# Down products of two SwiGLU blocks by Strassen's seven block products, with block sums on GpSimd, in a one-core decoder layer

## The chip, the cores and the metric

One NeuronCore of one Trainium2 chip. The metric is device microseconds (us) of one execution, input load and output store included. TensorE is called PE, VectorE DVE, ScalarE ACT, GpSimd POOL; SP issues the weight DMAs.

## What is computed

One layer on 256 tokens, width 1024, all float32: `x += 0.5*SwiGLU(RMSNorm(x))`, then a mixer (one input projection, 8 attention heads, 16 state-space heads, an output projection), then again `x += 0.5*SwiGLU(RMSNorm(x))` and a final RMSNorm. The part that changes is

```python
def swiglu(h, w1, w3, w2):
    return (jax.nn.silu(h @ w1) * (h @ w3)) @ w2
```

with h 256x1024, w1 and w3 1024x2816, w2 2816x1024, which runs twice (FFN n = 0 and 1, called FFN 1 and 2 in the text).

## The kernel before

**Products in three parts.** Every large product keeps float32 accuracy by splitting both operands in a high part (type fp32r) and the rest: `three` (L1112) issues hi*hi, hi*lo and lo*hi into one PSUM bank. So a weight that was loaded goes through two engines: ACT writes `w_hi` as a copy with the rounding type (`split_hi`, L453), DVE writes `w_lo` as raw minus high part (`split_lo`, L769), and `half_ready` counts the finished halves (128x1024 each), which PE waits for.

**Tiles and loops.** The 2816 hidden columns are 22 f-tiles of 128, taken in 11 pairs i = 0 to 10, odd = 0 or 1 within a pair. Three loads of 1 MB belong to a pair: w1 (kind 0), w3 (kind 1), w2 (kind 2), each into its own one of three raw slots (`ffn_load`, L268), issued on SP's queue in the order kind 0, 1, 2 and each once the second half that last lay in that slot is split. For f-tile (i, odd) PE computes gate and up, transposed, as 8 contraction tiles x 3 matmuls of 256 columns each (`gate_or_up`, L1149), into two banks: gate in bank 4, up in bank 5. ACT takes the silu of gate (`gate`, L500), DVE multiplies by up (`up`, L826), ACT and DVE split the product into `gu_hi` and `gu_lo`. PE then adds the f-tile's down product (`down`, L1133): two token tiles t x two column halves c, 3 matmuls of 512 columns each, accumulated in banks 0 to 3 over all 22 f-tiles. Pair 0 is different: both its f-tiles are computed with tokens on partitions (`pair_product`), multiplied, and transposed by PE (`pair_transposes`).

**Order of the work.** It is written out by hand on each engine; between engines there are only semaphores. PE does gate, up of one f-tile, then the down product of the f-tile before it (L1211 to L1217 is the loop over i). ACT and DVE run one `ffn_step` (L510, L837) for each f-tile: the splits of the next f-tile's w1 and w3, then silu and multiply, then the split of w2's half. A gate product waits only for its weights and for the silu before to have left bank 4.

On ACT:

```python
def ffn_step(n, i, odd):
    i2, odd2 = (i, 1) if not odd else (i + 1, 0)
    ffn_hi(n, i2, odd2, 0)
    ffn_hi(n, i2, odd2, 1)
    gate(n, i, odd)
    act.wait_ge(down_done, (FT - 1) * n + 2 * i + odd)
    ffn_hi(n, i2, odd2, 2)
```

At the end of an FFN `update_x` (L783, DVE) adds half of each finished bank to x. POOL does only small work: the norms' `rsqrt` (L363), nine parameter loads (L408 to L416) after the sixth down product, softplus, rotary products, and a 128x512 product in the mixer (L431).

## Time and profile before

| | |
|---|---|
| runs before | 572.85, 573.39, 572.8 us, median 572.85 |
| the profiled execution | 573.44 us, its span 571.7 us |
| PE busy | 553.1 us, 97% of the span |
| DVE, ACT, POOL busy | 324.1, 288.8, 49.3 us |
| DMA | 98.14 MB, mean 172 GB/s |

The profile is of one execution. The span runs from its first to its last instruction; 1.7 us of the execution's time lie outside. A row of a timeline gives start, duration, engine, line of the kernel, operation, output and inputs, and in brackets how long the engine sat idle before and who released it. PE's matmuls overlap, so the distance of starts, not the duration, is a matmul's price.

### The profile page before, as it was taken

To read this page: it belongs to the slowest core of one execution; us is meant where nothing else is said; L and a number is where in the kernel's file an instruction comes from. 1 tells how busy PE (TensorE), PEld (TensorE's weight loads), DVE (VectorE), ACT (ScalarE), POOL (GpSimd) and SP (SyncE) were. 2 spreads that over 40 slices of the span, in tenths; PEclk is the share of its full clock that TensorE was granted. 3 is DMA by queue.
4 is the path that set the end of the run, shared out by engine and by line. 5 is a ranking of instruction groups with operands and counts; after the bars stand their busy time and mean duration, and the time that the engine had idled before them with its cause. 6 is when DMAs were issued, how large, how long until landed. Compare 5 with 4: busy or idle time off the path is not lost.

```text
span 571.7 us, 9567 instructions
## 1 busy us (share of the span) xinstructions
PE 553.1 (97%) x3736; PEld 508.1 (89%) x3736; DVE 324.1 (57%) x450; ACT 288.8 (51%) x463; POOL 49.3 (9%) x86
## 2 busy tenths in 40 slices
PE   5999999999999999999999999999999999999994
PEld 4999999999999979998889688789999999999993
DVE  3655554554554684877766666575554544554544
ACT  4544453444443464866675874364453444443433
POOL 1000040000000020412431102010000000000001
PEclk9999999999999999999999999999999999999998
DMA  8935497655457637565323235253466655456601
GB/s 246 330 109 197 154 288 277 205 163 173 151 189 221 218 123 214 159 209 163 134 77 145 73 111 175 84 169 125 162 209 220 204 163 174 150 189 220 220 1 74
DMA packets 69448, 98.14 MB, mean 172 GB/s; under 512 B 1828, under 2 KB 55264, under 8 KB 69424
## 3 DMA queue, kind: packets, MB, share of 16 engines
q1 hardware_dynamic: 68576, 95.34, 51.7%
q0 software_dynamic: 848, 2.47, 1.5%
q8 instruction: 16, 0.26, 0.2%
q14 instruction: 8, 0.07, 0.0%
HBM read 96.75 MB, written 1.05 MB: 171 GB/s over the span
## 4 chain that ended last, share of the span: by engine, by line
PE 89%; DVE 4%; ACT 3%; DMA 1%; issue 1%; POOL 1%; SPq 0%; POOLq 0%; DVEq 0%; ACTq 0%
PE bank L1114 28%; PE bank L1115 27%; PE bank L1116 27%; DMA raw<-in_ffn_w 1%; PE bank L1239 1%; ACT decay L649 1%; DVE w_lo L775 1%; ACT z_silu L481 1%; ACT w_hi L457 1%; POOL mean_sq L368 1%; DVE x L787 1%; PE bank L1388 1%; PE bank L1387 1%; PE bank L1374 1%; DVE normed L992 0%
## 5 line engine op out<-in xcount | busy, mean ns | idle before, releaser
L775 DVE TENSOR_TENSOR w_lo<-raw,w_hi 128x1024 fp32r<-128x1024 f32 x176 | 211.1, 1228 | 146.0 <-ACT w_hi L457 145.5
L457 ACT ACTIVATE w_hi<-raw 128x1024 fp32r<-128x1024 f32 x176 | 179.6, 1054 | 114.6 <-PE bank L1116 73.2
L1114 PE MATMUL bank<-hT_hi,w_hi 128*128 128x256 f32 x736 | 208.5, 283 | 0.0
L1116 PE MATMUL bank<-hT_hi,w_lo 128*128 128x256 f32 x736 | 208.3, 283 | 0.0
L1115 PE MATMUL bank<-hT_lo,w_hi 128*128 128x256 f32 x736 | 208.2, 283 | 0.0
L1114 PEld LDWEIGHTS bank<-hT_hi,w_hi 128*128 128x128 f32 x736 | 141.1, 192 | 1.5
L1115 PEld LDWEIGHTS bank<-hT_lo,w_hi 128*128 128x128 f32 x736 | 141.1, 192 | 1.5
L1116 PEld LDWEIGHTS bank<-hT_hi,w_lo 128*128 128x128 f32 x736 | 141.1, 192 | 0.0
L1114 PE MATMUL bank<-w_hi,hT_hi 128*128 128x512 f32 (+1 forms) x192 | 70.1, 365 | 0.8 <-DVE w_lo L775 0.5
L1114 PE MATMUL bank<-w_hi,gu_hi 128*128 128x512 f32 x176 | 69.2, 393 | 0.3
L1115 PE MATMUL bank<-w_lo,gu_hi 128*128 128x512 f32 x176 | 69.0, 392 | 0.0
L1116 PE MATMUL bank<-w_hi,gu_lo 128*128 128x512 f32 x176 | 68.5, 389 | 0.0
L1116 PE MATMUL bank<-w_hi,hT_lo 128*128 128x512 f32 (+1 forms) x192 | 68.3, 356 | 0.0
L1115 PE MATMUL bank<-w_lo,hT_hi 128*128 128x512 f32 (+1 forms) x192 | 68.1, 354 | 0.0
L508 ACT ACTIVATE gu_hi<-gu 128x256 fp32r<-128x256 f32 x40 | 16.7, 418 | 89.1 <-DVE gu L832 83.4
L1114 PEld LDWEIGHTS bank<-w_hi,hT_hi 128*128 128x128 f32 x192 | 36.3, 189 | 7.7 <-issue 2.0
L1116 PEld LDWEIGHTS bank<-w_hi,hT_lo 128*128 128x128 f32 x192 | 36.3, 189 | 5.4
L1115 PEld LDWEIGHTS bank<-w_lo,hT_hi 128*128 128x128 f32 x192 | 36.3, 189 | 4.3
L1116 PEld LDWEIGHTS bank<-w_hi,gu_lo 128*128 128x128 f32 x176 | 33.1, 188 | 7.2
L1114 PEld LDWEIGHTS bank<-w_hi,gu_hi 128*128 128x128 f32 x176 | 33.2, 189 | 6.8 <-issue 1.1
L1115 PEld LDWEIGHTS bank<-w_lo,gu_hi 128*128 128x128 f32 x176 | 33.2, 189 | 5.3
L368 POOL TENSOR_SCALAR mean_sq<-sumsq 128x1 f32<-128x1 f32 x8 | 4.8, 596 | 346.6 <-ACT z_silu L481 346.6
(164 smaller groups left out, 413.6 us busy)
## 6 DMA issues: line engine op xcount, KB each, us to landing
raw<-in_ffn_w SPq DMA_DIRECT2D x63, 1024.0 KB, 5.5
raw<-in_w_in SPq DMA_DIRECT2D x16, 1024.0 KB, 5.6
raw<-in_w_out SPq DMA_DIRECT2D x6, 1024.0 KB, 4.9
raw<-in_ffn_w SPq DMA_DIRECT2D x6, 512.0 KB, 7.4
x<-in_x SPq DMA_DIRECT2D x4, 256.0 KB, 4.0
out_x<-normed SPq DMA_DIRECT2D x4, 256.0 KB, 2.0
norm_w<-in_ffn_norm SPq DMA_DIRECT2D x1, 512.0 KB, 6.3
norm_w<-in_mix_norm POOLq DMA_DIRECT2D x1, 512.0 KB, 6.4
```

Of the source, the lines that this page charges most:

```text
L368: step(pool.tensor_scalar(m, sumsq[:, 0, col:col + 1], sumsq[:, 1, col:col + 1], EPS, ALU.add, ALU.add))
L457: act.activation(by_tile(dst) if columns else dst, src, ACT.Copy).then_inc(hi_ready, 1)
L481: act.activation(z_silu[:, t, cols], x[:, t, cols], ACT.Square, scale=D ** -0.5, accum_out=sumsq[:, c, r:r + 1]).then_inc(sq_ready, 1)
L508: act.activation(gu_hi[:, odd, :], gu[:, :], ACT.Copy).then_inc(gu_hi_ready, 1)
L649: act.activation(probs[:, h % 2, a:b], probs[:, h % 2, a:b], ACT.Exp, bias=row_bias[:, h, t:t + 1], scale=HD ** -0.5, accum_out=row_sum[:, ...
L775: dve.tensor_tensor(lo, src, hi, ALU.subtract).then_inc(half_ready, 1)
L787: dve.scalar_tensor_tensor(xs, bank[:, 2 * t + c, :], 1.0 if n == 2 else 0.5, xs, ALU.mult, ALU.add).then_inc(x_ready, 1)
L1114: pe.matmul(dst, lhs[0], rhs[0], start=start, stop=False, skip_group_check=True)
L1115: pe.matmul(dst, lhs[0], rhs[1], start=False, stop=False, skip_group_check=True)
L1116: return pe.matmul(dst, lhs[1], rhs[0], start=False, stop=stop, skip_group_check=True)
L1239: last = pe.transpose(bank[:, bank_n, k * P:(k + 1) * P], normed[:, t, col + k * P:col + (k + 1) * P], ident)
L1374: pe.matmul(b[:, 0:384], select_r[:, h:h + 1].to_broadcast([P, P]), csT[:, :], start=True, stop=False, skip_group_check=True)
```

## The change

For the first ten pairs of an FFN, the pair's down product is seen as a 2x2 block product: A11, A12, A21, A22 (token tile t x f-tile, 128x128 each, out of `gu`) times B11, B12, B21, B22 (f-tile x 512 columns, out of w2). Strassen's scheme in Winograd's form needs seven block products instead of eight, with four sums of A blocks (S1 to S4) and four of B blocks (T1 to T4). The eleventh pair keeps eight products.

- POOL computes T1 to T4 out of the raw w2 tile once it is loaded (`pair_sums`, 128x512 each, T2 after T1, T4 after T2) and S1 to S4 out of `gu` (`operand_sums`, 128x128 each).
- ACT and DVE split what enters the products: B11 with B21 (`left`), T4 (`sum4`), T1 to T3 (`sums`), B22 (`corner`), S1 to S4 (`asum`). w1 and w3 are split as before; w2's halves only for the last pair.
- PE adds the seven products of all ten pairs into banks 4, 0, 1, 2, 5, 6, 7. Gate and up now share bank 3: a gate product waits until DVE has multiplied the f-tile before it (`gu_ready`), and the silu waits for up. Down products run in two parts (`down_first`: 3 products, `down_second`: 4), a pair late.
- The w2 load of a pair waits for `corner_ready` of the pair before; SP's loop issues the two loads of pair i+1, then w2 of pair i.
- At the end the seven sums are folded: a copy of one bank on ACT, four half-bank steps on DVE, and four additions to x on POOL (`fold`), while PE does the last pair. `update_x` waits for `folded` as well.
- POOL's nine parameter loads stand behind the sums of the second pair. `xbc`, `qT`, `kT` share memory with the new tiles; `gu`, `w2_sum` and `asum` lie in tiles of the mixer.

```diff
-PAIR_ORDER = ((0, 0), (0, 1), (1, 0), (1, 1), (0, 2), (1, 2))
+PAIR_ORDER = ((0, 0), (0, 1), (1, 0), (1, 1))
+PAIRS = FI - 1
+P_BANK = {1: 4, 2: 0, 3: 1, 4: 2, 5: 5, 6: 6, 7: 7}
+GU_BANK = 3
...
+            def w2_load(n, i):
+                sp.wait_ge(corner_ready, i + PAIRS * n)
+                ffn_load(sp, n, i, 2)
...
+                gate_up_loads(n, 1)
+                with sp.Fori(1, FI - 1) as i:
+                    gate_up_loads(n, i + 1)
+                    w2_load(n, i)
...
+            def pair_sums(n, i):
+                p, w = PAIRS * n + i, w2_blocks(n)
+                pool.wait_ge(raw_loaded[(FFN_UNIT0[n] + 2) % RAW_SLOTS], w2_count(n, i))
+                if not (isinstance(p, int) and p == 0):
+                    pool.wait_ge(sums_ready, p)
+                    pool.wait_ge(sum4_ready, p)
+                pool.tensor_tensor(w2_sum[:, T1, :], w[:, 1, :], w[:, 0, :], ALU.subtract).then_inc(sum_done, 1)
+                pool.wait_ge(sum_done, p * 4 + 1)
+                pool.tensor_tensor(w2_sum[:, T2, :], w[:, 3, :], w2_sum[:, T1, :], ALU.subtract).then_inc(sum_done, 1)
+                pool.wait_ge(sum_done, p * 4 + 2)
+                pool.tensor_tensor(w2_sum[:, T4, :], w[:, 2, :], w2_sum[:, T2, :], ALU.subtract).then_inc(sum_done, 1)
+                pool.tensor_tensor(w2_sum[:, T3, :], w[:, 3, :], w[:, 1, :], ALU.subtract).then_inc(sum_done, 1)
...
+            def silu(n, i, odd):
+                f = looped(n, i, odd)
+                act.wait_ge(up_done, f + 1)
+                act.activation(silu_g, bank[:, GU_BANK, 0:SEQ], ACT.Silu).then_inc(silu_ready, 1)
...
+            def ffn_step(n, i):
+                second_hi(n, i - 1)
+                act.wait_ge(gate_done, looped(n, i, 0) + 1)
+                ffn_hi(n, i + 1, 0, 0)
+                silu(n, i, 0)
+                ffn_hi(n, i + 1, 0, 1)
+                product_hi(n, i, 0)
+                left_hi(n, i)
+                sum4_hi(n, i)
+                act.wait_ge(gate_done, looped(n, i, 1) + 1)
+                ffn_hi(n, i + 1, 1, 0)
+                silu(n, i, 1)
+                ffn_hi(n, i + 1, 1, 1)
+                product_hi(n, i, 1)
...
                 ffn_hi(n, 1, 0, 1)
+                left_hi(n, 0)
                 act.wait_ge(pair_T, 2 * n + 2)
...
+                act.activation(gu_hi[:, :, :], both, ACT.Copy)
+                act.activation(gu, both, ACT.Copy).then_inc(pair_copied, 1)
+                sum4_hi(n, 0)
                 ffn_hi(n, 1, 1, 0)
                 ffn_hi(n, 1, 1, 1)
...
+            def ffn_step(n, i):
+                second_lo(n, i - 1)
+                ffn_lo(n, i + 1, 0, 0)
+                up_silu(n, i, 0)
+                ffn_lo(n, i + 1, 0, 1)
+                product_lo(n, i, 0)
+                left_lo(n, i)
+                sum4_lo(n, i)
+                ffn_lo(n, i + 1, 1, 0)
+                up_silu(n, i, 1)
+                ffn_lo(n, i + 1, 1, 1)
+                product_lo(n, i, 1)
...
             def gate_or_up(n, i, odd, kind):
...
+                if kind == 0 and not (isinstance(f, int) and f == 0):
+                    pe.wait_ge(gu_ready, f)
+                columns_product(slot, bank[:, GU_BANK, kind * SEQ:(kind + 1) * SEQ]).then_inc(up_done if kind else gate_done, 1)
+
+            def gate_up_down(n, i):
+                gate_or_up(n, i, 0, 0)
+                if isinstance(i, int) and i == 1:
+                    for t in range(TT):
+                        pair_transposes(n, t)
+                gate_or_up(n, i, 0, 1)
+                down_first(n, i - 1)
+                gate_or_up(n, i, 1, 0)
+                gate_or_up(n, i, 1, 1)
+                down_second(n, i - 1)
```

In the text, hi(i,odd,gate) and lo(i,odd,gate) are the splits of w1's half (i, odd) on ACT and DVE, gate(i,odd) is PE's product; a tile or function name with _hi or _lo is its split.

## Rows read from the trace of the kernel before

**Rows 1.** The page, busy time, share of the span and instructions of each engine.
```profile
PE 553.1 (97%) x3736; PEld 508.1 (89%) x3736; DVE 324.1 (57%) x450; ACT 288.8 (51%) x463; POOL 49.3 (9%) x86
```

**Rows 2.** The page, chain that ended last, share of the span by engine.
```profile
PE 89%; DVE 4%; ACT 3%; DMA 1%; issue 1%; POOL 1%; SPq 0%; POOLq 0%; DVEq 0%; ACTq 0%
```

**Rows 3.** Timeline of PE, second FFN, steady step: start us, us, instruction.
```profile
442.29 0.28 PE L1114 MATMUL bank<-hT_hi,w_hi 128*128 128x256 f32 x1
448.04 0.40 PE L1114 MATMUL bank<-w_hi,gu_hi 128*128 128x512 f32 x1
450.79 0.28 PE L1114 MATMUL bank<-hT_hi,w_hi 128*128 128x256 f32 x1
```

**Rows 4.** The page, costliest groups: line, engine, forms, count, busy us, mean ns, idle before.
```profile
L775 DVE TENSOR_TENSOR w_lo<-raw,w_hi 128x1024 fp32r<-128x1024 f32 x176 | 211.1, 1228 | 146.0 <-ACT w_hi L457 145.5
L457 ACT ACTIVATE w_hi<-raw 128x1024 fp32r<-128x1024 f32 x176 | 179.6, 1054 | 114.6 <-PE bank L1116 73.2
```

**Rows 5.** Instructions by line or tile: count, duration ns min/median/max, first and last start.
```profile
L832 DVE TENSOR_TENSOR gu<-bank,conv_acc x40: 417/425/425, 35.6 to 558.7; 128x256 f32<-128x256 f32 x40
L431 POOL TENSOR_TENSOR normed<-x_tok,small x4: 1042/1194/2022, 265.3 to 271.6; 128x512 f32<-128x512 f32 x4
L602 ACT ACTIVATE q_tok<-bank x2: 617/622/626, 273.6 to 274.1; 128x512 f32<-128x512 f32 x2
```

**Rows 6.** Timeline of SP's queue, second FFN: three weight loads issued.
```profile
446.20 0.37 SPq L280 DMA_DIRECT2D raw<-in_ffn_w  x1
447.18 0.37 SPq L280 DMA_DIRECT2D raw<-in_ffn_w  x1
453.55 0.37 SPq L280 DMA_DIRECT2D raw<-in_ffn_w  x1
```

**Rows 7.** DMA issues 446:447, 447:449, 449:454, in this order: KB, us to landing.
```profile
raw<-in_ffn_w SPq DMA_DIRECT2D x1, 1024.0 KB, 5.5
raw<-in_ffn_w SPq DMA_DIRECT2D x1, 1024.0 KB, 7.5
raw<-in_ffn_w SPq DMA_DIRECT2D x1, 1024.0 KB, 5.0
```

**Rows 8.** Timeline of DVE and POOL in the mixer.
```profile
294.60 1.34 DVE L775 TENSOR_TENSOR w_lo<-raw,w_hi 128x1024 fp32r<-128x1024 f32 x1
294.94 1.32 POOL L382 TENSOR_TENSOR k_tok<-k_tok,cst 128x128 f32<-128x128 f32 x1
299.21 0.53 POOL L382 TENSOR_TENSOR k_tok<-k_tok,cst 128x128 f32<-128x128 f32 x1
...
269.59 2.05 POOL L431 TENSOR_TENSOR normed<-x_tok,small 128x512 f32<-128x512 f32 x2 [2.93 <-ACT x_tok L622]
270.98 1.74 DVE L775 TENSOR_TENSOR w_lo<-raw,w_hi 128x1024 fp32r<-128x1024 f32 x1 [1.86 <-ACT w_hi L457]
```

**Rows 9.** Timeline of PE and ACT, first FFN: first pair, and its last matmul.
```profile
28.24 0.28 PE L1114 MATMUL bank<-hT_hi,w_hi 128*128 128x256 f32 x1
31.76 0.60 ACT L534 ACTIVATE gu_hi<-bank 128x512 fp32r<-128x512 f32 x1 [1.99 <-PE bank L1178]
34.43 0.40 PE L1114 MATMUL bank<-w_hi,gu_hi 128*128 128x512 f32 x1
...
204.30 0.39 PE L1116 MATMUL bank<-w_hi,gu_lo 128*128 128x512 f32 x1
```

**Rows 10.** The page, DMA queues: packets, MB, share of 16 engines.
```profile
q1 hardware_dynamic: 68576, 95.34, 51.7%
q0 software_dynamic: 848, 2.47, 1.5%
```

**Rows 11.** PE's last matmul, then two stretches (granted clock third from the end).
```profile
564.16 0.39 PE L1116 MATMUL bank<-w_hi,gu_lo 128*128 128x512 f32 x1
...
566.00:568.00 2.00, 0.00 (x0) 0.00 (x0) 1.16 (x3) 0.95 (x3) 1.39 (x2) 0.74 0.58 218
568.00:570.00 2.00, 0.00 (x0) 0.00 (x0) 0.20 (x1) 0.42 (x1) 0.00 (x0) 0.50 0.60 224
```

More of the change, by code:

```diff
@@ L418, in _ @@
+            fold(0)
             pool.wait_ge(scaled_right, 2)
@@ L519, in pair_silu, with last_step @@
+            def last_step(n):
+                i = FI - 1
+                second_hi(n, i - 1)
+                silu(n, i, 0)
+                product_hi(n, i, 0)
+                for j in range(2):
+                    last_hi(n, j)
+                fold_copy(n)
+                if n == 0:
+                    mix_hi(0)
+                silu(n, i, 1)
+                product_hi(n, i, 1)
             def pair_silu(n, t):
@@ L744, in _ @@
             norm_hi(2, 1)
-            for odd in range(2):
-                ffn_hi(1, 0, odd, 2)
             ffn_steps(1)
-            gate(1, FI - 1, 1)
             for c in range(2):
@@ L845, in pair_mul, with last_step @@
+            def last_step(n):
+                i = FI - 1
+                second_lo(n, i - 1)
+                up_silu(n, i, 0)
+                product_lo(n, i, 0)
+                for j in range(2):
+                    last_lo(n, j)
+                if n == 0:
+                    mix_lo(0)
+                up_silu(n, i, 1)
+                product_lo(n, i, 1)
+                fold_sums(n)
             def pair_mul(n, t):
@@ L1140, in down_both, with down_last @@
+            def down_last(n):
+                pe.wait_ge(last_ready, 2 * n + 2)
+                pe.wait_ge(gu_split, FT * (n + 1))
                 for t in range(TT):
                     for c in range(2):
-                        last = down(n, i, odd, t, c, start, False)
-                last.then_inc(down_done, 1)
-            def down_waits(n, i, odd):
-                pe.wait_ge(half_ready, ffn_half(n, i, odd, 2)[0] + 1)
-                pe.wait_ge(gu_split, FT * n + 2 * i + odd + 1)
+                        for j in range(2):
+                            slot = FFN_SLOT[n][j]
+                            last = three(bank[:, 2 * t + c, :], (gu_hi[:, j, tok(t)], gu_lo[:, j, tok(t)]),
+                                         tuple(w[:, slot, c * 512:(c + 1) * 512] for w in (w_hi, w_lo)),
+                                         t + c + 1 - j == 3, j == 1)
+                        last.then_inc(acc_ready, 1)
```

394 lines of the change are left out of this document (244 added, 150 removed).

## The prediction

> **What bounds the kernel now.** I read three views in this order. The page's busy shares put the matmul engine PE at 97% of the span, VectorE (DVE) at 57%, ScalarE (ACT) at 51%, GpSimd (POOL) at 9% [rows 1]; the chain of waits gives PE 89% of what ended last [rows 2]. So outside the norms the kernel is PE's own instruction stream. The PE timeline of one steady step gives its prices [rows 3]: from 442.29 to 448.04 two products (gate, up) of 24 matmuls of 256 columns run, so 2.875 us a product, 0.120 us a matmul; from 448.04 to 450.79 twelve matmuls of 512 columns, 0.229 us each. A pair of f-tiles is two such steps: 4 x 2.875 + 24 x 0.229 = 17.0 us. Everything else, 6 weight splits of 1.06 us on ACT and 1.23 us on DVE a pair [rows 4], hides under it.
>
> **What the change takes off PE.** Seven block products instead of eight, three matmuls each: 3 x 0.229 = 0.687 us less a pair, so 16.3 us. Ten pairs an FFN, two FFNs: -13.7 us. If nothing else moved, that were the result.
>
> **What it adds, and which ring it closes.** Per pair: on POOL four sums of 128x512 and four of 128x128; on ACT and DVE, for the two w2 halves split before, hi/lo splits of B11 with B21 (1024 columns), T4 (512), T1 to T3 (1536), B22 (512) and the operand sums (512). The nearest POOL row to a sum of 128x512 is a 128x512 product, 1.042 us at least and 1.19 in the median [rows 5]; I take 1.04, and keep 1.34 as the upper end for a sum with two full streams (below). Scaled by columns from 1.23, DVE gets 4 x 1.23 for gate and up, 4.9 for the new splits, 1.7 for two multiplies and two subtractions of 0.42 [rows 5]: 11.5 of 16.3 us. ACT fits as well. Busy time is thus no bound; order is.
>
> ACT's order in a step is: hi(i+1,0,gate), silu, hi(i+1,0,up), gu_hi, left_hi, sum4_hi, hi(i+1,1,gate), silu(i,1), and so on. sum4_hi waits for POOL's third sum T4, T4 for the w2 load of this pair, and everything behind it on ACT waits too, at last silu(i,1), whose multiply frees the one gate/up bank for gate(i+1,0). The loads are on one queue and every raw slot is single. The gate load i+2 is issued when lo(i+1,1,gate) is done, the up load a split later, the w2 load of i+1 when corner_lo of pair i is done, some 5 us on. In the trace the first two were issued at 446.20 and 447.18 [rows 6] and landed after 5.5 and 7.5 us [rows 7], at 451.7 and 454.7: they go one after the other, 3.0 us apart. A w2 load alone lands in 5.0 us [rows 7], so with the same start-up as the gate load (5.5 - 3.0 = 2.5) it moves for some 2.5 to 2.6 us; third in the stream, it lands 8.5 + 2.6 = 11.1 us after the gate load's issue. Then the ring, from the gate load's issue to the next one's: three loads 11.1; T1, T2, T4 in series with a semaphore between, 3 x 1.04 + 0.2 = 3.3; sum4_hi 0.6 [rows 5], less the overlap with its successor, 0.55; hi(.,1,gate) 1.06; lo 1.28 with its wait [rows 4]; issue 0.05. That is 17.3 us, and PE isn't in it. It is already longer than the 16.3 PE needs, and than the 17.0 of before, where the w2 split did not stand in front of a silu with POOL sums before it.
>
> **The port that POOL and DVE share.** left_lo, a DVE subtraction of two SBUF tiles, comes due just as T1 ends and T2 starts. The trace shows what two such instructions do side by side: a POOL 128x128 product took 1.32 us at 294.94, beside a DVE split that ran 294.60 to 295.94, and 0.53 us at 299.21; the other way round a DVE split took 1.74 us at 270.98 instead of 1.23, having waited for a POOL product that ended at 271.6 [rows 8]. One waits for the other to finish. So either T2 waits for left_lo or T4 does: 1.23 less some overlap, 1.0 us, and the ring is 18.3. The Trainium skill (SBUF — State Buffer, section on two separate sides) says that a DVE instruction with two SBUF inputs and a GpSimd instruction exclude each other for the whole instruction; by that rule the trace agrees, and the sum stays 18.3. The Trainium skill (GPSIMD Engine Reference, performance versus the Vector engine) gives 2.6 cycles an element at 1.2 GHz for two-input sums, an estimate of 1.11 us; with it the ring would be 0.2 us longer.
>
> Excess over PE's 16.3: 2.0 us in each of the 8 full rounds (from gate(2,0) to gate(10,0)): +16.0 an FFN.
>
> **The first step.** In FFN 1 gate(1,0) starts at 28.24 and the pair's transposed product is read by ACT at 31.76 [rows 9]. Behind it ACT now has a second copy, sum4_hi and hi(1,1,gate): 31.76 + 3 x 0.5 + 1.06, then lo 1.28: the next gate load is issued at 35.6, with the port 36.0, and lands at 41.5. hi(2,0,gate) stands on ACT ahead of silu(1,0), and lo ahead of the multiply on DVE: 41.5 + 1.06 + 1.28 + 0.4 + 0.15 = 44.4 before gate(1,1) may write the shared bank. PE, which reached its first down product at 34.43 [rows 9], is through nine matmuls at 36.5: 7.9 us idle, where before it had another bank. The third load of this stream lands at 47.1; 4.3 for three sums with the port, 0.55 + 1.06 + 1.28 + 0.57 put gate(2,0) at 54.9, 26.6 us after gate(1,0); PE's own work there (four products, 0.45 of transposes, 21 matmuls of 0.229) is 16.8. So +9.8.
> The last step costs +0.5 (all waits of the last down product now stand in front). The fold, four DVE steps of 0.7 and four POOL sums of 1.04, lies beside the last 5.5 us of down product and ends before the last block; cover gone, it would cost up to 2 us. It is taken at 0.
>
> Per FFN: -6.9 + 16.0 + 9.8 + 0.5 = +19.4; two, +38.8. An FFN lasts 176.3 us now (28.24 to 204.55 [rows 9]), so 195.7 after.
>
> **Smaller terms.** POOL's parameter loads move behind the second pair's sums into a stretch where weights stream: all of that queue's packets took 1.5% of 16 engines' span [rows 10], 8.6 us, about half of them these loads; +2, between 0 and 4.5. PE's clock: after the last matmuls at 564.2 the granted clock was 0.74 of 2.4 GHz in 566 to 568 and 0.50, so 1.2 GHz, after it [rows 11]. A gap of 7.9 us thus lowers it; one product at half rate (2.9 more) fits in the slack before silu(1,1) but for 0.3, two would cost 3.2. I take 0.5 each. The mixer is as before but for slots: 0.
>
> Sum against the profiled execution: 573.4 + 38.8 + 2 + 1 = 615.2; the median of the runs is 0.6 lower, so 614.6. I say **614**.
>
> **Rivals.** (A) The forecast, a ring of three loads, three sums and two splits with the port: 600 to 628, chance 0.57.
> (B) The port costs nothing on the ring, because the sums slip between splits or the sum stream holds it less: per FFN 8 x 1.0 + 0.8 less, so 614 - 17.6 = 596. Against it: both stretched rows. The range of this case is 586 to 600 (a load lands 0.4 us sooner: another -4 a FFN). The Trainium skill (Perfetto Trace Analysis, optimizing scalar/DVE operations) names only a 2-port DVE instruction as holder of the lock; a subtraction that were not one would give this 596, and [rows 8] speak against it. Chance 0.18.
> (C) Faster: the ring doesn't close, since loads and sums of a pair run ahead of PE; then PE's 16.3 stands and the time is 572.9 - 13.7 = 559. It decides at a ring of 16.3 (1.0 below my ring without the port) and a first gap under 6.9 us, which alone eats the saving; both have to give way. For it: the transfers are busy only half the time, 51.7% [rows 10]. Against: three single slots and the measured 5.5, 7.5 and 5.0 us. Chance 0.07 (with values between 559 and 571).
> (D) A sum with two full streams is dearer than the one of [rows 5]: 1.34 us instead of 1.04 adds 0.9 to each of nine rounds, +8 to 9 an FFN: 631. For it: the product's second input is one value repeated. Chance 0.16.
> (E) The saving and the waits cancel, or the change isn't what runs: 573, chance 0.02.
>
> **Numbers.** 614 is the likeliest case's. The range 591 to 631 holds most of A, B's centre and about half of D. A measurement of this kernel tells some 0.2% (1.1 us) from no change. Slower 0.92 (A, B, D and a bit), same 0.01, faster 0.07.
>
> **What the profile will show.** If right: PE idle in front of every gate(i,0), 1.5 us or more, released by DVE's multiply and behind it ACT's sum4_hi, POOL's T4 and a w2 load; rounds of 18.3 us; one gap near 8 us in each FFN's first step; w2 loads landing 6 us after issue; PE's share near 89%; POOL sums of 1.04 beside some of 2 us. Wrong if PE is still near 97%, if rounds are 16.3, if T1 starts well before ACT reaches left_hi, or if no POOL sum is stretched (then B).

## The result, and the profile after

The kernel with the block products takes 651.8 us (median of 4 runs, 648.72 to 654.32) where before takes 572.83 (572.77 to 573.39): a ratio of 1.137, 95% interval 1.132 to 1.142. The forecast was 614 with a range to 631: the direction is right, the size is not, and the measurement lies 21 us outside the range. The profiled execution took 652.08 us, with a span of 650.5.

The page of after; the first line answers to [rows 1], the shares of the chain to [rows 2], the last three lines are groups (count, busy us, mean ns, idle before):

```profile
PE 569.1 (87%) x3676; PEld 517.9 (80%) x3676; DVE 404.4 (62%) x518; ACT 334.1 (51%) x527; POOL 269.6 (41%) x254
PEclk9989899989989799999999999997988999889988
...
PE 28%; DVE 16%; issue 16%; POOL 16%; DMA 13%; ACT 9%; POOLq 0%; SPq 0%; ACTq 0%; DVEq 0%
...
L464 POOL TENSOR_TENSOR x_tok<-raw 128x512 f32<-128x512 f32 x20 | 25.9, 1294 | 138.2 <-DMA raw<-in_ffn_w 138.2
L628 ACT ACTIVATE w_hi<-x_tok 128x512 fp32r<-128x512 f32 x20 | 12.6, 632 | 71.6 <-POOL x_tok L468 71.6
L466 POOL TENSOR_TENSOR x_tok<-raw,x_tok 128x512 f32<-128x512 f32 x20 | 41.4, 2070 | 1.6
```

No engine is full, and the chain is spread over all of them: PE's part fell from 89% to 28%. That is the picture of a ring, a closed chain of waits in which the last link releases the first. x_tok holds the sums T1 to T4 here, v_tok holds gu. The waits of after (engine and line, what it waited for: us in total, times, longest us) name its links:

```profile
POOL x_tok L464 <- DMA raw<-in_ffn_w: 138.2, 19, 11.5
DVE w_lo L938 <- ACT w_hi L568: 73.1, 60, 3.2
ACT w_hi L628 <- POOL x_tok L468: 71.6, 18, 4.1
PE bank L1331 <- DVE v_tok L1039: 58.1, 20, 7.5
DVE w_lo L998 <- ACT w_hi L628: 57.8, 18, 3.2
```

T1 waits for the w2 load; sum4_hi (L628) waits for T4 (L468); and PE waits 20 times for DVE's multiply (L1039), once in front of every gate(i,0) from i = 2 on (0.8 to 4.0 us) and once in each first step (7.3 and 7.5 us).

One round of FFN 1, in order of time, from the timeline: ACT, DVE, POOL and the gate product's first matmul. The gate load was issued at 137.51, the up load at 138.82, the w2 load at 142.78; they landed after 5.6, 7.2 and 5.8 us, so the third at 148.58. The next gate load was issued at 156.66.

```profile
137.71 0.39 PE L1331 MATMUL bank<-hT_hi,w_hi 128*128 128x256 f32 x1 [4.01 <-DVE v_tok L1039]
139.67 2.07 DVE L1004 TENSOR_TENSOR sums_lo<-x_tok,sums_hi 128x1536 fp32r<-128x1536 f32 x1 [0.28 <-ACT sums_hi L636]
141.66 0.94 DVE L1007 TENSOR_TENSOR w_lo<-raw,w_hi 128x512 fp32r<-128x512 f32 x1
148.65 1.29 POOL L464 TENSOR_TENSOR x_tok<-raw 128x512 f32<-128x512 f32 x1 [6.58 <-DMA raw<-in_ffn_w]
149.69 1.33 DVE L993 TENSOR_TENSOR w_lo<-raw,w_hi 128x1024 fp32r<-128x1024 f32 x1 [0.96 <-ACT w_hi L621]
150.02 2.15 POOL L466 TENSOR_TENSOR x_tok<-raw,x_tok 128x512 f32<-128x512 f32 x1
152.25 1.29 POOL L468 TENSOR_TENSOR x_tok<-raw,x_tok 128x512 f32<-128x512 f32 x1
153.58 0.63 ACT L628 ACTIVATE w_hi<-x_tok 128x512 fp32r<-128x512 f32 x1 [3.91 <-POOL x_tok L468]
154.11 1.04 ACT L568 ACTIVATE w_hi<-raw 128x1024 fp32r<-128x1024 f32 x1
154.24 1.11 DVE L998 TENSOR_TENSOR w_lo<-x_tok,w_hi 128x512 fp32r<-128x512 f32 x1 [3.22 <-ACT w_hi L628]
155.28 1.21 DVE L938 TENSOR_TENSOR w_lo<-raw,w_hi 128x1024 fp32r<-128x1024 f32 x1
156.88 0.39 PE L1331 MATMUL bank<-hT_hi,w_hi 128*128 128x256 f32 x1 [1.10 <-DVE v_tok L1039]
```

This is the ring of the forecast, link by link: 11.07 us from the gate load's issue to the third landing, 4.96 to T4's end (153.54), then 3.12 for sum4_hi, sum4_lo, lo(.,1,gate) and the issue, together 19.15. This round is the shortest of FFN 1. Gate(2,0) to gate(10,0) is 56.43 to 217.88, 20.18 a round, and the three loads take 12.1 us in the mean of the eight (11.1 to 12.6). The rows on either side of T2 (L466) show the port: T2 took 2.15 where its neighbours took 1.29, beside left_lo (L993).

Two more places of after. The first step's gaps answer to [rows 9] (gate(1,1) and gate(2,0)), and the end of FFN 1 has the norm's transposes at 245.42, where before has them at 205.35:

```profile
44.66 0.55 PE L1331 MATMUL bank<-hT_hi,w_hi 128*128 128x256 f32 x1 [7.27 <-DVE v_tok L1039]
56.43 0.39 PE L1331 MATMUL bank<-hT_hi,w_hi 128*128 128x256 f32 x1 [0.96 <-DVE v_tok L1039]
...
217.88 0.55 PE L1331 MATMUL bank<-hT_hi,w_hi 128*128 128x256 f32 x1 [3.91 <-DVE v_tok L1039]
245.42 1.09 PE L1463 MATMUL bank<-cst,normed 128*128 128x128 f32 x8 [2.86 <-DVE normed L978]
```

The last step, in ACT's, DVE's and POOL's timelines. The silu(10,1) (L654) stands behind the copy for the fold (L649) and a mixer split, but its bracket shows that it waited for PE, so they did not delay it. The updates of x (L952) stand behind a second mixer split that the fold's GpSimd sums (L501) stretched from 1.23 to 2.31 us:

```profile
231.44 0.58 ACT L649 ACTIVATE x_tok<-bank 128x512 f32<-128x512 f32 x1
231.91 1.05 ACT L568 ACTIVATE w_hi<-raw 128x1024 fp32r<-128x1024 f32 x1
234.18 0.39 ACT L654 ACTIVATE conv_acc<-bank 128x256 f32<-128x256 f32 x1 [1.22 <-PE bank L1333]
...
239.22 2.31 DVE L938 TENSOR_TENSOR w_lo<-raw,w_hi 128x1024 fp32r<-128x1024 f32 x1
241.46 1.28 DVE L952 SCALAR_TENSOR_TENSOR x<-bank,x 128x512 f32<-128x512 f32 x2
...
237.86 4.82 POOL L501 TENSOR_TENSOR x<-x_tok,x 128x512 f32<-128x512 f32 x3 [3.73 <-DVE x_tok L1021]
```

### The profile page after: what moved, and what is told of

Read it like the earlier page. It is cut to its first block, busy times and chain, and to the rows that moved or that the text cites. A ratio compares the mean times of both kernels' runs of the same rounds, so it can differ in the third digit from the quotient of the medians.

```text
span 650.5 us, 9885 instructions
## 1 busy us (share of the span) xinstructions
PE 569.1 (87%) x3676; PEld 517.9 (80%) x3676; DVE 404.4 (62%) x518; ACT 334.1 (51%) x527; POOL 269.6 (41%) x254
## 4 chain that ended last, share of the span: by engine, by line
PE 28%; DVE 16%; issue 16%; POOL 16%; DMA 13%; ACT 9%; POOLq 0%; SPq 0%; ACTq 0%; DVEq 0%
DMA raw<-in_ffn_w 13%; PE bank L1331 8%; PE bank L1333 7%; PE bank L1332 7%; POOL x_tok L466 6%; DVE sums_lo L1004 5%; ACT sums_hi L636 4%; POOL x_tok L468 4%; POOL x_tok L464 4%; DVE w_lo L938 3%; ACT w_hi L628 2%; DVE w_lo L1007 1%; DVE v_tok L1039 1%; ACT decay L815 1%; PE bank L1463 1%
## 5 line engine op out<-in xcount | busy, mean ns | idle before, releaser
L1331 PE MATMUL bank<-hT_hi,w_hi 128*128 128x256 f32 x736 | 221.9, 302 | 58.2 <-DVE v_tok L1039 58.1
L938 DVE TENSOR_TENSOR w_lo<-raw,w_hi 128x1024 fp32r<-128x1024 f32 x132 | 165.8, 1260 | 73.7 <-ACT w_hi L568 73.1
L568 ACT ACTIVATE w_hi<-raw 128x1024 fp32r<-128x1024 f32 x132 | 138.3, 1053 | 56.9 <-DMA raw<-in_ffn_w 43.3
L1332 PEld LDWEIGHTS bank<-hT_lo,w_hi 128*128 128x128 f32 x736 | 151.6, 206 | 0.4
L464 POOL TENSOR_TENSOR x_tok<-raw 128x512 f32<-128x512 f32 x20 | 25.9, 1294 | 138.2 <-DMA raw<-in_ffn_w 138.2
L998 DVE TENSOR_TENSOR w_lo<-x_tok,w_hi 128x512 fp32r<-128x512 f32 x20 | 21.6, 1079 | 57.8 <-ACT w_hi L628 57.8
L481 POOL TENSOR_TENSOR q_tok<-v_tok 128x128 f32<-128x128 f32 x20 | 25.6, 1281 | 57.8 <-DVE v_tok L1039 37.7
L628 ACT ACTIVATE w_hi<-x_tok 128x512 fp32r<-128x512 f32 x20 | 12.6, 632 | 71.6 <-POOL x_tok L468 71.6
L993 DVE TENSOR_TENSOR w_lo<-raw,w_hi 128x1024 fp32r<-128x1024 f32 x20 | 27.5, 1377 | 24.9 <-ACT w_hi L621 24.9
L466 POOL TENSOR_TENSOR x_tok<-raw,x_tok 128x512 f32<-128x512 f32 x20 | 41.4, 2070 | 1.6
L1004 DVE TENSOR_TENSOR sums_lo<-x_tok,sums_hi 128x1536 fp32r<-128x1536 f32 x20 | 37.5, 1876 | 4.0 <-ACT sums_hi L636 3.5
L621 ACT ACTIVATE w_hi<-raw 128x1024 fp32r<-128x1024 f32 x20 | 21.2, 1058 | 26.9 <-DMA raw<-in_ffn_w 26.9
```

The lines of the kernel that those rows point to most:

```text
L464: pool.tensor_tensor(w2_sum[:, T1, :], w[:, 1, :], w[:, 0, :], ALU.subtract).then_inc(sum_done, 1)
L466: pool.tensor_tensor(w2_sum[:, T2, :], w[:, 3, :], w2_sum[:, T1, :], ALU.subtract).then_inc(sum_done, 1)
L568: act.activation(by_tile(dst) if columns else dst, src, ACT.Copy).then_inc(hi_ready, 1)
L628: act.activation(w_hi[:, SPLIT_REST, 0:512], w2_sum[:, T4, :], ACT.Copy).then_inc(sum4_hi_ready, 1)
L938: dve.tensor_tensor(lo, src, hi, ALU.subtract).then_inc(half_ready, 1)
L993: dve.tensor_tensor(in_two(w_lo[:, SPLIT_LEFT, :]), w2_blocks(n)[:, 0:3:2, :], in_two(w_hi[:, SPLIT_LEFT, :].bitcast(f32)), ALU.subtract). ...
```

## The experiments

A gap in this section is the distance from one matmul's start to the next one's; the idle time in a row's bracket is 0.3 to 0.4 us shorter. The theory going in: the ring of loads, GpSimd sums and splits, in which PE has no part, sets the rounds, and its terms were under-priced. Rivals: the bank that gate and up now share; ACT's or DVE's own time; the loads alone. Times are medians, ratios are to before on the same chip.

### The saving alone

Kernel before, with the last three matmuls of each pair's down product left out; part of the product is missing.

```
                     for c in range(2):
+                        if odd == 1 and t == 1 and c == 1:
+                            continue
                         last = down(n, i, odd, t, c, start, False)
```

> The kernel before, with one of the eight block products of each of the first ten pairs of both FFNs left out (token tile 1, column half 1 of the second f-tile, 3 matmuls of 512 columns); that part of the sum is missing from the output. It prices the saving alone, with no sums and no new order. Both theories: 20 pairs x 3 x 0.229 us = 13.7 us less, 559 us. If the time stays near 573, PE's matmuls aren't what bounds the kernel before and the whole first step of my forecast falls.

Measured: 559.56 us, ratio 0.976 (0.973 to 0.979), where 559 was forecast. What seven products for eight take off PE is 13.7 us, as worked out. Everything over 559.6 in after, 92 us, is the form in which they come.

### The sums made short

Kernel after, the four GpSimd sums over 32 of 512 columns; the rest of T1 to T4 is not the sum.

```
-pool.tensor_tensor(w2_sum[:, T1, :], w[:, 1, :], w[:, 0, :], ...)
+pool.tensor_tensor(w2_sum[:, T1, 0:32], w[:, 1, 0:32], w[:, 0, 0:32], ...)
```

> The changed kernel, with POOL's four w2 sums (T1 to T4) over 32 of their 512 columns (the rest stays zero or old, so those sums are missing); same waits, same splits. Ring theory (three loads, sums T1 T2 T4, sum4 split, gate split, next load make the round of 20.2 us): T1 to the end of T4 lasts 4.9 us now and would last about 1.3, so the ring falls to 16.6 and PE's own 16.3 nearly binds: 8 rounds x 3.6 x 2 = -58 and 2 x 3.6 in the first steps, about 587 us, round 16.6. Rival, the shared gate/up bank (PE waits for silu and multiply whatever the sums do): rounds stay near 20, 645 to 652 us.

Measured: 586.29 us, ratio 1.023 (1.020 to 1.026). The rounds fell from 20.2 to 16.3 us (gate(8,0), gate(9,0) and gate(10,0) began at 154.41, 170.72 and 187.03), and in the loop PE is idle for at most 0.1 us in front of a gate product. So PE's own 16.3 is the floor as forecast, and the sums' time with its port is worth 65 us of the 92. What is left over 559.6 is 27 us. Two first-step gaps of 7.9 are 16 of it, and the product behind each ran at a lowered clock (gate(1,1) to its up product 5.26 us instead of 2.97), 4.6 more; the tail of FFN 1 has 2.2 more behind the last matmul than before has. The rest was not traced. Whether a GpSimd instruction with one input instead of two would be stretched as well was not measured.

### Banks of their own

Kernel after, gate and up in banks 2 and 3 with silu behind gate alone, product 4 added in bank 0.

```
-P_BANK = {1: 4, 2: 0, 3: 1, 4: 2, 5: 5, 6: 6, 7: 7}
+P_BANK = {1: 4, 2: 0, 3: 1, 4: 0, 5: 5, 6: 6, 7: 7}
...
-columns_product(slot, bank[:, GU_BANK, kind * SEQ:(kind + 1) * SEQ])
+columns_product(slot, bank[:, 2 + kind, 0:SEQ])
```

> The changed kernel with gate and up in banks of their own, as before the change: the fourth block product is added into the second one's bank (so the output mixes two products), gate waits only for the silu to have left its bank, the silu only for gate. Ring theory: the ring has no bank in it (loads, sums, splits), so rounds stay at 20 us and the time within 645 to 652; only the gaps move to other places. Rival, the shared bank: gate(i+1,0) no longer waits for the multiply, rounds fall to PE's 16.3 to 17, 590 us or less.

Measured: 652.13 us, ratio 1.138 (1.134 to 1.142): no change. The waits show PE idle as long as before, now for ACT's silu (L654), which stands behind the same sum4_hi:

```profile
PE bank L1334 <- ACT conv_acc L654: 56.7, 22, 6.3
```

The shared bank decides which instruction PE is seen waiting for, not how long.

### One split moved out of the ring

Kernel after, T4's split behind the second silu and multiply.

```
     left_hi(n, i)
-    sum4_hi(n, i)
     act.wait_ge(gate_done, looped(n, i, 1) + 1)
     ffn_hi(n, i + 1, 1, 0)
     silu(n, i, 1)
+    sum4_hi(n, i)
```

> The changed kernel with one move: the split of T4 stands behind the second silu (ACT) and behind the second multiply (DVE) of its step instead of in front of the gate split of the next pair. Nothing is left out. Ring theory: the gate load no longer waits for T1, T2, T4; the next longest ring is w2's own (w2 load, sums, split of T1 to T3, corner split, next w2 load, with the port shared), which I work out at 1.1 us less than now: rounds about 19, 8 x 1.1 x 2 = -18 and some 2 x 2 in the first steps, 630 us. Rival, DVE and POOL are full because they share a port (a resource, not an order): no change, 648 to 654. Rival, PE's slow clock: no change either unless the gaps close.

Measured: 608.52 us, ratio 1.062 (1.059 to 1.065), rounds of 17.5 us. It took 43 us off, where 22 was expected: the move opens the ring instead of shortening it. Gate and w2 loads no longer queue behind each other (in the steady rounds a w2 load lands 4.7 to 5.1 us after its issue), and another ring is the likely limit; no run cuts that ring alone. It is in DVE's, POOL's and ACT's timelines of one round; the w2 load was issued at 149.09 and landed at 153.95:

```profile
154.02 1.30 POOL L464 TENSOR_TENSOR x_tok<-raw 128x512 f32<-128x512 f32 x1 [5.65 <-DMA raw<-in_ffn_w]
155.40 2.16 POOL L466 TENSOR_TENSOR x_tok<-raw,x_tok 128x512 f32<-128x512 f32 x1
157.63 2.15 POOL L468 TENSOR_TENSOR x_tok<-raw,x_tok 128x512 f32<-128x512 f32 x1
...
156.33 2.31 DVE L938 TENSOR_TENSOR w_lo<-raw,w_hi 128x1024 fp32r<-128x1024 f32 x1
163.53 2.01 DVE L1004 TENSOR_TENSOR sums_lo<-x_tok,sums_hi 128x1536 fp32r<-128x1536 f32 x1
165.47 0.95 DVE L1007 TENSOR_TENSOR w_lo<-raw,w_hi 128x512 fp32r<-128x512 f32 x1
```

Load 4.9, T1 to T4 5.8 with the port twice, then 6.8 for the splits up to the corner's (T4, a half of the next pair, the product, T1 to T3, the corner), and the next w2 load at 166.58: 17.5 us. A split of 1.23 us took 2.31 beside T2 and T4.

### Thin w2 loads

Kernel after, the w2 loads of pairs 1 to 9 cut to 64 of 1024 columns; the down product uses stale data there.

```
+if not (isinstance(i, int) and i in (0, FI - 1)):
+    src, dst = src[:, :, 0:64], dst[:, :, 0:64]
 eng.dma_start(dst, src).then_inc(raw_loaded[s], 16)
```

> The kernel after, with the w2 loads of pairs 1 to 9 of each FFN carrying 64 of their 1024 columns (the rest of the slot keeps stale data, so the down product is wrong there); number, order and waits of the loads unchanged. It asks whether the loads' transfer time is a term of the ring. Theory (three loads in series, 12.1 us of a 20.2 us round, of which the w2 load itself is some 2.6 to 3.0): w2 lands 2.3 to 2.8 us sooner, rounds of 17.4 to 17.9 us, time 652 - 16 x 2.5 = 612, with the first steps 608; between 602 and 616. Rival (the start-up of each load and the wait for corner_lo set the landing, not the bytes): less than 1 us a round, 636 to 650. Rival (the loads are hidden, and the engines' order alone makes the round): 650 to 652.

Measured: 618.23 us, ratio 1.078 (1.076 to 1.080), 2 us above the expected stretch, with rounds of 18.3. The load term moved as said: in one round the third load landed 9.2 us behind the gate load's issue (128.80 to 137.97), just behind the up load (137.80). In the mean of the sixteen rounds it was 9.2 where after has 12.0. But the rounds lost only 1.8 of these 2.8 us. The next rows, DVE's timeline in that round, show where one went back: with w2 there sooner, three splits met the sums, and sum4_lo (L1000) ended at 145.79, 2.8 us after T4; in after's round these are 1.8:

```profile
140.34 1.51 DVE L1045 TENSOR_TENSOR gu_lo<-v_tok,gu_hi 128x256 fp32r<-128x256 f32 x1
141.78 2.31 DVE L995 TENSOR_TENSOR w_lo<-raw,w_hi 128x1024 fp32r<-128x1024 f32 x1
144.01 1.78 DVE L1000 TENSOR_TENSOR w_lo<-x_tok,w_hi 128x512 fp32r<-128x512 f32 x1
```

### Corner first, operand sums later

The kernel with T4's split moved, and the corner split ahead of the sums T1 to T3, the operand sums' split behind the next first silu.

```
+act.activation(w_hi[:, SPLIT_REST, 512:1024], w2_blocks(n)[:, 3, :], ACT.Copy).then_inc(corner_hi_ready, 1)
 act.activation(sums_hi[:, :, :], w2_sum[:, T1:T3 + 1, :], ACT.Copy).then_inc(sums_hi_ready, 1)
...
     silu(n, i, 0)
     ffn_hi(n, i + 1, 0, 1)
+    operand_hi(n, i - 1)
     product_hi(n, i, 0)
```

> The kernel with T4's split behind the second silu (x4_sum4_after_silu, 608.5 us, rounds of 17.5), and two more changes of order in the loop: the corner block is split before the sums T1 to T3, so that the next w2 load is issued some 2 us sooner, and the split of the operand sums moves behind the first silu and multiply of the next step. The output is the reference's. In that run w2's own ring was load 4.9 + sums 5.8 + three splits on ACT and DVE in front of the next issue = 17.5 us. Theory (this second ring, again without PE, is what is left): the ring is cut to 15.5 us, PE's own 16.3 stands, rounds of 16.3 to 16.6, time 608.5 - 16 x 1.0 = 590 to 593; the first steps keep their gaps of 7.7 to 8 us and the tails theirs. Rival (PE waits for the multiply because DVE and ACT lack time of their own, not because of the order): rounds stay over 17.2, 604 to 609.

Measured: 611.99 us, ratio 1.067 (1.064 to 1.071): a miss, no better than 608.5, with rounds of 16.3 to 19.0. In its timeline PE waits at 143.34 for a multiply (L1045) that stood behind a split of 2.30 us (in after's round the split in that place took 1.21):

```profile
140.64 2.30 DVE L942 TENSOR_TENSOR w_lo<-raw,w_hi 128x1024 fp32r<-128x1024 f32 x1
142.87 0.41 DVE L1045 TENSOR_TENSOR v_tok<-bank,conv_acc 128x256 f32<-128x256 f32 x1
...
143.34 0.39 PE L1341 MATMUL bank<-hT_hi,w_hi 128*128 128x256 f32 x1 [1.39 <-DVE v_tok L1045]
```

The reading of this: the two rings were open, and what held the round now was DVE with what the port added to it. The groups of the gate and up splits bear it out: mean 1260 ns in after, 1445 here, so 132 of them took 24 us more.

```profile
L942 DVE TENSOR_TENSOR w_lo<-raw,w_hi 128x1024 fp32r<-128x1024 f32 x132 | 190.2, 1445 | 67.7 <-ACT w_hi L568 67.1
L468 POOL TENSOR_TENSOR x_tok<-raw,x_tok 128x512 f32<-128x512 f32 x20 | 42.1, 2103 | 1.6
```

### First and last step reordered too

The last kernel, with the first step written out and the tail in a new order.

> x7_order_corner_first with the first step and the last step reordered too. First step: silu and multiply of (1,0) and (1,1) stand ahead of the gate/up splits of pair 2, which wait for their load. Last step: the silu and the split of (10,1) stand ahead of the copy of product 1 for the fold, and the split of the mixer's second half stands behind the updates of x. The output is the reference's. Theory (the two gaps of 7.7 to 8 us are ACT's order and not the load itself; a second wait of some 3 us for the w2 load stays): -4 to -5 us a first step, -3 to -4 us a tail in FFN 1 and -2 in FFN 2, so 14 us less than x7: 576 to 580. If it goes better than that, at 571 or less, the scheme beats the kernel before (573). Rival (the first gap is the load's: gate(2,0) waits as long as gate(1,1) did): only the tails' 5 us, 586.

```
-                ffn_step(n, 1)
+                second_hi(n, 0)
+                silu(n, 1, 0)
+                operand_hi(n, 0)
+                product_hi(n, 1, 0)
+                ffn_hi(n, 2, 0, 0)
...
```

Measured: 613.94 us, ratio 1.068 (1.064 to 1.073): a miss, the same as the one before it. The gap of 7.9 us in front of gate(1,1) fell to 3.5, but one of 5.5 and one of 1.3 us came a step later, since the gate load of pair 3 was now issued at 57.27, behind a split that waited for w2. The wait moved on by one step.

### The sums on VectorE

Kernel after, T1, T2, T4 (`block_sums`) and T3 (`last_sum`) of all pairs but the first on DVE; nothing else changed.

```
     product_lo(n, i, 0)
+    block_sums(n, i)
     left_lo(n, i)
+    last_sum(n, i)
     sum4_lo(n, i)
```

> The kernel after, with the sums T1, T2, T4, T3 of every pair but the first of each FFN on VectorE instead of GpSimd, ahead of and behind its split of the left blocks; nothing else changed. The output is the reference's. A VectorE 128x512 instruction of two SBUF inputs took 0.69 us, so the three sums in the ring take 2.1 us where GpSimd took 4.9 with the shared port. Theory (the time and the port of the GpSimd sums are a term of the ring): rounds 20.2 - 2.8 = 17.4, time 652 - 16 x 2.8 = 607, between 600 and 614. Rival (VectorE has no room for 2.8 us more a round and its other work slips): rounds of 18.5 or more, 625 to 650.

Measured: 614.4 us, ratio 1.072 (1.069 to 1.076), at the expected stretch's upper end. The groups: a sum takes DVE half of what it takes POOL without a neighbour, and a third of what it took with one.

```profile
L997 DVE TENSOR_TENSOR x_tok<-raw,x_tok 128x512 f32<-128x512 f32 x18 | 12.5, 692 | 0.6
L1005 DVE TENSOR_TENSOR w_lo<-raw,w_hi 128x1024 fp32r<-128x1024 f32 x20 | 24.4, 1218 | 0.0
```

The left split is back at 1.218 us from 1.377. Rounds were 18.3 in FFN 1 and 17.6 in FFN 2; the loads took 12.5 and 11.8 us in the mean of each FFN's eight rounds. Why the loads of FFN 1 are slower was not found.

### New order and sums on VectorE

The loop of "corner first", and the sums on DVE.

> x7_order_corner_first (612 us) with the same move of the sums to VectorE. In its trace the bank was freed late because the split of (i+1,1,gate) ran beside a GpSimd sum (2.30 instead of 1.23 us) in front of the second multiply, and the first multiply stood behind splits stretched in the same way. Theory (what kept that order's rounds at 17.8 us is the port that GpSimd and VectorE share): with the sums on VectorE nothing is stretched there, rounds of 16.3 to 16.6, PE's own, time 612 - 16 x 1.3 = 591, between 586 and 594. Rival (VectorE, busy 14.6 of 16.3 us then, is itself the bound, or the order closes another ring): rounds stay at 17.3 or more, 603 or more.

Measured: 595.04 us, ratio 1.038 (1.036 to 1.039), 1 us above the expected stretch, with rounds of 16.4 to 17.5. Against the same order with the sums on GpSimd that is 17 us less, so the sums on GpSimd, and not the order alone, held that kernel. The run takes away both their own time and the port, and does not part the two. The mean of the 132 splits fell from 1445 to 1298 ns; most splits that are still stretched lie beside the four small operand sums that stay on POOL.

### The first two steps written out

The last kernel's loop, the reordered tail, and steps 1 and 2 of each FFN written out so that no silu or multiply stands behind a split that waits for a load.

```
     sum4_hi(n, 0)
     ffn_hi(n, 1, 1, 0)
+    silu(n, 1, 0)
     ffn_hi(n, 1, 1, 1)
...
+    ffn_hi(n, 2, 0, 0)
+    silu(n, 1, 1)
+    product_hi(n, 1, 1)
+    ffn_hi(n, 2, 0, 1)
```

> The loop of x12_order_and_vector_sums, the tail of x9_order_first_tail, and the first two steps of each FFN written out in an order in which no silu or multiply stands behind a split that waits for a load. The output is the reference's. x9 had two gaps there, 3.5 and 1.3 + 5.5 us, since the gate load of pair 3 was issued at 57.3, behind a split that waited for w2. Theory (the order alone makes these gaps): steps 1 and 2 cost PE 2 to 3 us in all instead of 8 to 10, so 591 - 2 x 6 - 5 = 574, between 568 and 580. Rival (the loads of the first steps can't come sooner, and the gaps stay): 586 to 590.

Measured: 589.11 us, ratio 1.027 (1.024 to 1.029), 9 us more than the expected stretch's upper end of 580. The first gap is gone, one of 2.1 us is left in front of pair 1's down product, which waits for its w2 load, and 1.4 + 3.8 us moved to step 3, where a multiply stood behind the split of a gate half whose load landed at 71.79. PE's rows with an idle time in 70 to 77 us:

```profile
70.41 0.49 PE L1407 MATMUL bank<-w_hi,gu_hi 128*128 128x512 f32 x1 [1.11 <-DVE w_lo L1037]
76.12 0.58 PE L1407 MATMUL bank<-hT_hi,w_hi 128*128 128x256 f32 x1 [3.36 <-DVE v_tok L1080]
```

### The tail alone

Kernel after with the last step's order alone changed.

```
     product_hi(n, i, 0)
+    if n == 0:
+        mix_hi(0)
     for j in range(2):
         last_hi(n, j)
-    fold_copy(n)
-    if n == 0:
-        mix_hi(0)
     silu(n, i, 1)
     product_hi(n, i, 1)
+    fold_copy(n)
```

> The kernel after with the last step's order alone changed, as in x9: the silu and the split of (10,1) ahead of the copy for the fold, the mixer's first half split ahead of the w2 halves, its second half behind the updates of x. The output is the reference's. The forecast took the last step at +0.5 and the fold at 0; the profile of after shows 27.5 us from gate(10,0) to the norm's transposes, where before took 20.9. Theory (4 of those 6.6 us in FFN 1 are ACT's and DVE's order behind the load of w2(10), and some 1 to 2 in FFN 2): 652 - 5 = 647, between 644 and 649. Rival (the wait is the w2 load and the fold itself): 651 to 653.

Measured: 654.68 us, ratio 1.143 (1.141 to 1.145): a miss, and no gain. Gate(10,0) to the norm's transposes did fall from 27.5 to 24.3 us, but most of this is not the order. In neither kernel is PE idle between gate(10,0) and its last matmul; in after gate(10,0) itself ran at half clock, behind an idle time of 3.9 us, and here at full clock, behind 1.5. Gate(10,0) to up(10,0) took 5.26 us there and 2.94 here, 2.3 us. The windows (granted clock third from the end), of after and then of this run:

```profile
218.00:223.00 5.00, 5.00 (x24) 5.00 (x25) 4.14 (x4) 2.46 (x4) 4.50 (x4) 0.50 0.85 279
220.00:222.60 2.60, 2.60 (x23) 2.60 (x24) 2.47 (x3) 2.06 (x3) 2.52 (x3) 1.00 0.70 176
```

The order is worth what fell behind the last matmul: its start to the transposes went from 3.45 to 2.64 us, 0.8. There the updates of x were now early (238.87), but the norm's POOL work stood behind the fold's sums, which ended at 241.89. The stretch from there to the next norm's transposes grew by 1.2 (165.1 to 166.3), where the moved split came later, and the rounds of this run were 0.2 us longer than in after, 16 times. Why the rounds were longer stays open.

### The corner first, alone

Kernel after, corner block split ahead of T1 to T3 on ACT and DVE.

```
+act.activation(w_hi[:, SPLIT_REST, 512:1024], w2_blocks(n)[:, 3, :], ACT.Copy).then_inc(corner_hi_ready, 1)
 act.activation(sums_hi[:, :, :], w2_sum[:, T1:T3 + 1, :], ACT.Copy).then_inc(sums_hi_ready, 1)
-act.activation(w_hi[:, SPLIT_REST, 512:1024], w2_blocks(n)[:, 3, :], ACT.Copy).then_inc(corner_hi_ready, 1)
```

> The kernel after, with the split of the corner block B22 ahead of the split of the sums T1 to T3 on ScalarE and VectorE, and nothing else: the w2 load, which in the profile of after is issued 5.3 us behind the gate load, goes out some 2 us sooner. The output is the reference's. The forecast's term for the loads was that the three go one after the other and the third lands 11.1 us behind the gate load's issue; after showed 11.1 to 12.7. Theory (the transfers are in series: w2 lands 2.6 to 3.5 us behind up, whenever it is issued): the landing moves by 0 to 0.8 us, rounds of 19.6 to 20.2, 640 to 652. Rival (the landing is the w2 issue plus its own 5.8 us): 1.5 to 2 us sooner, rounds of 18.3 to 18.8, 620 to 628.

Measured: 644.52 us, ratio 1.125 (1.123 to 1.128), inside the expected stretch. The w2 load went out 2.9 us behind the gate load instead of 5.3 (FFN 1) and 4.9 (FFN 2), and landed 8.1 to 9.6 us after its issue instead of 5.8 to 7.6. The means of each FFN's eight rounds, in us behind the gate load's issue:

| | up load lands | w2 load lands | round |
|---|---|---|---|
| forecast | 8.5 | 11.1 | 18.3 |
| after, FFN 1 and 2 | 8.9, 9.0 | 12.1, 11.8 | 20.2, 20.1 |
| this run, FFN 1 and 2 | 8.8, 9.1 | 11.4, 11.6 | 19.5, 19.9 |

Issued early, the w2 load lands 2.5 to 2.6 us behind the up load, as forecast, and the rounds lose what the landing gains, 0.7 us in FFN 1 and 0.2 in FFN 2. So the late issue is a part of the missing term, 0.7 of 1.0 us and 0.2 of 0.7. The other part is that the up load itself lands 0.3 to 0.6 us later than the forecast's 8.5, and why stays open.

### The w2 loads on a second queue

Kernel after, the w2 loads of pairs 1 to 10 issued by ACT.

```
+def w2_load(n, i):
+    act.wait_ge(corner_ready, i + PAIRS * n)
+    ffn_load(act, n, i, 2)
```

> The kernel after, with the w2 loads of pairs 1 to 10 issued by ScalarE on its own queue, behind its split of the operand sums, instead of by SyncE; issued at about the same time, some 5.5 us behind the gate load. The output is the reference's. It asks whether the w2 load lands late (5.8 to 7.3 us after its issue, against 5.0 to 5.6 alone) because it stands behind the up load in one queue, or because the three share the 16 engines. Theory (the engines are shared: one queue or two, the last of three 1 MB loads lands at the same time): rounds of 20 to 20.5, 648 to 656. Rival (order within the one queue): the w2 load lands 5.0 to 5.6 us after its issue, but the up load no later: 1 us a round less, 634 to 638.

Measured: 655.64 us, ratio 1.145 (1.142 to 1.147). One w2 load was issued at 144.21 and landed 6.6 us on, 11.9 behind the gate load's issue at 138.93; in the mean of the sixteen rounds the third load landed 12.1 us behind that issue, and 12.0 in after. So the one queue was not what delayed it. That the three share the same 16 engines fits this, but no run shows it by itself.

### The third step written out too

The kernel of "The first two steps written out", with step 3 of each FFN in such an order as well.

> x11_order_vector_first_tail (589 us) with the third step of each FFN written out too, its first silu and multiply ahead of the splits of pair 4. In x11 the multiply of (3,0) stood behind the split of a gate half whose load landed at 71.75, and PE waited 1.4 + 3.8 us there in FFN 1 and 0.9 + 3.8 in FFN 2. The output is the reference's. Theory (these gaps are order): -4 us an FFN, 581, between 578 and 583. Rival (the late loads move the gap on to the next step): 586 to 590. It doesn't beat the kernel before by either; what is left over 559.6 (the products alone) is then VectorE's 14.6 of 16.3 us a round, the w2 load of the first steps and the tails.

```
     second_hi(n, 2)
+    silu(n, 3, 0)
     ffn_hi(n, 4, 0, 0)
     ffn_hi(n, 4, 0, 1)
```

Measured: 592.54 us (589.21 to 594.67, 6 runs), ratio 1.037 (1.035 to 1.038): a miss, 3 us slower than without it if anything. The gap of 3.8 us fell to 2.7, and others of 1.0 appeared behind it. No kernel of this study with the block products beats before; the best, 589, is 2.7% slower.

## Why the prediction was wrong

The mechanism stands, and its price was too low. Step by step:

**Products and saving** (16.3 a pair, -13.7 us): right. 559.56 measured for 559, and 16.31 us rounds once the ring is out of the way.

**The ring**, 18.3 us forecast, 20.18 measured in FFN 1 and 20.06 in FFN 2 (gate(2,0) 459.36 to gate(10,0) 619.80), with three terms short. *Loads*: 11.1 forecast, 12.1 in the mean of FFN 1 and 11.8 in FFN 2. The first step that failed is that the third load lands 11.1 us after the gate load's issue although it goes out "some 5 us on". With an issue 4.9 to 5.3 us behind the gate load's, one round of FFN 1 came to 11.1 and the others to 11.6 to 12.6. Issued 2.9 us behind, the means were 11.4 and 11.6, so the rest, the later landing of the up load, was mis-sized too and its cause is open. *Sums*: 3.3 + 1.0 for the port forecast, 4.9 measured. The 1.04 us taken from the least of [rows 5] is 1.29 without a neighbour; of the values weighed, the upper end, 1.34, was the right one. The port term, 1.0, came out at 0.86 (2.15 less 1.29), so it was right. *Splits behind T4*: 2.9 forecast, 3.1 measured. Here sum4_lo took 1.11 us where a split of its size takes 0.69 alone, beside T3; that was no term of the sum, since only T2 or T4 was taken to meet a DVE split. It is worth about 0.1 us, for the next split could not have begun before its high part was done at 155.15. Taken together, from the third landing to the next gate load's issue 8.07 us pass in FFN 1 and 8.21 in FFN 2, where the forecast has 7.2. With the loads that is 1.85 and 1.7 us a round for 1.88 and 1.76 measured, 29 us over 16 rounds.

**PE isn't in it**: right, and shown from both sides: the sums made short give 16.3, another bank gives nothing.

**First step**: gate(1,1) was forecast at 44.4 and came at 44.66; gate(2,0) at 54.9, came at 56.43. The gap and its cause were right, the 1.5 us are again the late third load and the sums.

**Last step and fold** (+0.5, and 0 with "cover gone up to 2"): the second failed step. By the sum on record FFN 1's last matmul ends at 28.24 + 195.7 = 223.9, which leaves 223.9 - 54.9 - 8 x 18.3 = 22.6 us behind gate(10,0), 23.4 with the 0.8 to the transposes that before had; 27.5 were measured, 4.1 more. The last matmul ended after 24.3 us, 1.7 over the forecast, with PE idle nowhere in between: the half clock in gate(10,0) took 2.3, a term that the forecast had for the first step only. The other 2.4 lie behind it, 3.2 us to the transposes instead of 0.8. The forecast had the fold end before the last block; its last three sums, 1.04 us each in the forecast, took 4.82 together (L501) and ended at 242.68, behind the last matmul's end at 242.2, and the mixer's second split, stretched to 2.31 by them, stood in front of the updates of x. The run with another order got back 0.8 of these. In FFN 2 gate(10,0) to the last matmul's end took 23.2 us, 0.6 over the forecast, with 1.3 by the clock (gate(10,0) to up(10,0) 4.28 us).

**Second FFN's start**, taken at 0: T1 to T4 of pair 0 run on POOL beside DVE's norm work (1.27, 1.34, 2.14, 1.27 us from 417.56 on). The norm's second transposes follow the first by 8.6 us (410.55 to 419.17) where before has 7.7, and from there the pair's transposes come after 15.3 us (434.51) where before has 12.7: +3.5. The run with the short sums has 7.7 and 12.8 there, so the sums cost it. In part they do it by way of the clock: behind idle times of 1.9 and 1.1 us the first product took 4.5 us instead of 3.0, at a granted 0.63 in 421.4 to 426.

**Parameter loads +2, clock +1**: no run separates the loads, and the account below leaves no room for them. The clock cost more than 1 us, 2.3 + 1.3 in the last steps and 1.5 in the second FFN's start, which is counted in those terms; inside the ring it cost nothing that shows. The granted clock was 0.950 over the span, and PE's idle time of 4.0 us before 137.71 was followed by 0.57 of 2.4 GHz in 138 to 142 (1.2 GHz would be 0.50). The windows (as [rows 11], granted clock third from the end):

```profile
133.00:137.70 4.70, 0.70 (x4) 0.22 (x2) 2.59 (x4) 2.80 (x5) 2.56 (x3) 1.00 0.00 0
138.00:142.00 4.00, 4.00 (x23) 4.00 (x23) 3.72 (x4) 2.11 (x3) 3.92 (x4) 0.57 0.78 255
142.00:150.00 8.00, 8.00 (x61) 7.63 (x61) 4.82 (x7) 4.61 (x6) 1.36 (x2) 1.00 0.76 266
```

The clock came back to full speed and the round still ended with PE waiting, so the loss lies inside the ring's slack. The forecast had the clock fall in the first step's gaps only; it fell in some rounds as well.

**The account.** The spans differ by 650.5 - 571.7 = 78.8, forecast were 41.8, so 37 are missing: ring 29.1, first steps 2.7, FFN 1's last step 4.1, FFN 2's start 3.5 and last step 0.6, less the 3 taken for parameter loads and for the clock, which is counted in the other terms: 37.0. That it closes so well is in part luck, since no term is known better than to some tenths. The range failed at its upper end: 631 priced a dear sum alone, and the load term, the last step and the second start had no upper ends of their own.

**Rivals.** B (the port costs nothing, 596) falls: T2 took 2.07 us in the mean, T1 1.29. The Trainium skill (SBUF — State Buffer, the section on two separate sides) has it that a DVE instruction with two SBUF inputs and a GpSimd one exclude each other. The traces agree, in both directions: T2, begun behind left_lo, took 2.15 us for 1.29, and a split begun behind T2 took 2.31 for 1.23. C (559) falls with the ring. D (dear sums) was right in its row, 1.29 for an upper end of 1.34, and 631 was still too low.
